# Reordering the loads at the end of two mixture-of-experts stages

## The reference

```
h  = modulate(rms_norm(x, norm_mix), sh1, sc1);  u = split_cols(h @ w_in)      # w_in: 1024 x 2400
x  = x + g1 * (concat(gqa, neighbourhood, differential, latent attention)(u) @ w_out)
h2 = modulate(rms_norm(x, norm_ffn), sh2, sc2)
x  = x + g2 * moe_ffn(h2)
moe_ffn(h) = swiglu(h; shared expert) + sum over 16 experts e: gates[:, e] * swiglu(h; expert e)   # top 2 of 16
swiglu(x, wg, wu, wd) = (silu(x @ wg) * (x @ wu)) @ wd                           # 1024 x 256, 1024 x 256, 256 x 1024
```

## Time and profile before

| | |
|---|---|
| runs | 1728.34, 1732.85, 1733.67 us |
| profiled execution | 1731.82 us, its span 1730.0 us |
| busy shares | TensorE 90%, VectorE 48%, ScalarE 26%, POOL 11% |
| mean granted TensorE clock | 0.966 |
| blocks of layer 0, of layer 1 (us from the start) | about 722 to 964, 1505 to 1696 |

### The profile page before, as it was taken

One profiled execution on the slowest core, in us unless ns is written; L12 is line 12 of the kernel. 1 busy time (PEld: TensorE's weight loads), 2 busy tenths in 40 slices (PEclk: granted clock), 3 DMA queues, 4 the chain that ended last, 5 costly groups with the idle time before them and its releaser, 6 DMA issues.

```text
span 1730.0 us, 24248 instructions
## 1 busy us (share of the span) xinstructions
PE 1561.9 (90%) x8946; PEld 1020.6 (59%) x8946; DVE 827.1 (48%) x1749; ACT 444.1 (26%) x970; POOL 192.8 (11%) x350
## 2 busy tenths in 40 slices
PE   3999999899999999799999489999899999799991
PEld 3655446665665487577677255555565657477771
DVE  1122524567666475255555422434667655444444
ACT  1412113454544210000000142113545531000001
POOL 0110102000000000012211111202000000112112
PEclk7999999999999999899999699999999999899996
DMA  9574230501001589778888820232301123678884
GB/s 336 186 262 146 99 49 1 183 1 38 15 33 40 196 325 390 274 298 316 326 306 314 322 104 4 87 55 63 122 1 37 38 94 128 238 280 305 331 320 165
DMA packets 110485, 295.25 MB, mean 171 GB/s; under 512 B 32568, under 2 KB 42230, under 8 KB 95990
## 3 DMA queue, kind: packets, MB, share of 16 engines
q1 hardware_dynamic: 100022, 272.96, 44.5%
q0 software_dynamic: 10368, 20.99, 3.3%
HBM read 270.72 MB, written 44.04 MB: 182 GB/s over the span
## 4 chain that ended last, share of the span: by engine, by line
PE 82%; DMA 7%; DVE 3%; issue 3%; ACT 3%; SPq 2%; POOL 0%; POOLq 0%; DVEq 0%; ACTq 0%
PE S L1186 16%; PE S L1505 13%; PE B L1319 9%; PE S L1254 9%; PE S L1515 6%; PE PT L1271 5%; PE B L1302 5%; DMA arena<-in_moe_w_up 3%; PE B L1205 3%; PE B L1101 2%; ACT arena L859 2%; PE PT L1499 2%; PE S L1205 2%; PE S L1384 1%; PE PT L1408 1%
## 5 line engine op out<-in xcount | busy, mean ns | idle before, releaser
L1186 PE MATMUL S<-arena 128*128 128x512 f32 (+3 forms) x768 | 301.9, 542 | 13.0 <-ACT arena L859 13.0
L1505 PE MATMUL S<-arena 128*128 128x256 f32 x1152 | 261.3, 384 | 7.2 <-DMA arena<-in_moe_w_up 4.9
L1505 PEld LDWEIGHTS S<-arena 128*128 128x128 f32 x1152 | 220.1, 192 | 55.8 <-issue 27.1
L1186 PEld LDWEIGHTS S<-arena 128*128 128x128 f32 x768 | 141.2, 193 | 137.6 <-issue 105.5
L971 ACT ACTIVATE arena<-S,nmax 128x768 f32<-128x768 f32 (+1 forms) x200 | 161.8, 812 | 159.9 <-DVE nmax L1929 119.7
L1929 DVE TENSOR_REDUCE nmax<-S 128x1 f32<-128x768 f32 (+1 forms) x168 | 133.1, 825 | 84.7 <-PE S L1254 84.5
L1254 PE MATMUL S<-arena 64*128 64x256 f32 (+5 forms) x720 | 161.7, 499 | 9.7 <-ACT arena L971 7.9
L1319 PE MATMUL B<-arena 128*128 128x512 f32 x320 | 156.0, 617 | 2.9 <-DVE arena L1983 2.1
L1271 PEld LDWEIGHTS PT<-cst,arena 128*128 128x128 f32 x832 | 94.0, 141 | 84.2 <-issue 65.4
L1271 PE MATMUL PT<-cst,arena 128*128 128x128 f32 x832 | 121.0, 277 | 24.4 <-ACT arena L971 11.7
L1515 PE MATMUL S<-arena 128*128 128x512 f32 x288 | 129.9, 594 | 2.4 <-DVE arena L2067 2.4
(11 more groups left out here) (282 smaller groups left out, 1703.0 us busy)
## 6 DMA issues: line engine op xcount, KB each, us to landing
arena<-in_w_mod SPq DMA_DIRECT2D x24, 2048.0 KB, 13.3
arena<-in_moe_w_gate SPq DMA_DIRECT2D x36, 1024.0 KB, 5.9
arena<-in_moe_w_up SPq DMA_DIRECT2D x36, 1024.0 KB, 8.9
arena<-in_moe_w_down SPq DMA_DIRECT2D x36, 1024.0 KB
arena<-in_w_in SPq DMA_DIRECT2D x6, 2048.0 KB, 8.4
arena<-y SPq DMA_DIRECT2D x20, 512.0 KB, 7.9
arena<-mod SPq DMA_DIRECT2D x16, 512.0 KB, 16.0
arena<-in_tokens SPq DMA_DIRECT2D x12, 512.0 KB, 9.4
```

Source lines behind the costliest of these rows:

```text
L1186: mm = pe.matmul(ubank[u % 4][:, c0:PANEL_W[p]], hT[:, k, t * P:(t + 1) * P], panel[p][:, k, c0:], start=k == 0, stop=k == KT - 1)
L1505: mm = pe.matmul((S0, S1)[b][:, 512 * w:512 * w + DE], XT[b][:, k, :], wgu[b][:, w, k * DE:(k + 1) * DE], start=k == 0, stop=k == KT - 1)
```

## The change

On SP, in both layers: the loop over `w_load` is split. Blocks 2 and 3 are asked for first, then the residual rows (3 MiB in six loads in layer 0; 2 MiB in four and the gain of 0.5 MiB in layer 1), then in layer 0 panel 0, a wait for `e_y` at 1 (the first block's result scaled), and panel 1, and only then the loop over the weights of blocks 4 and on. `spare_pairs` moves from ahead of the loads of `y` to behind them. In layer 0 the stores to `x_in` wait until all six tiles are summed.

```diff
@@ -794,14 +794,8 @@
                 if l == 0:
                     gain_load(1)
                     mod_store(1)
-                with sp.Fori(0, pairs_1) as i:
-                    for b in range(2):
-
-                        w_load(2 * i + 2 + b, b)
-                if l == 0:
-
-                    win_load(1, 0)
-
+                for b in range(2):
+                    w_load(2 + b, b)
                 for b in range(2):
                     sp.wait_ge(s[f"s_stored{b}"], 8 * gend if l == 0 else 16 * (T // 2 + TL // 2))
                 sp.wait_ge(s["s_d"], gend)
@@ -810,13 +804,18 @@
                 if l == DEPTH - 1:
                     sp.dma_start(fgain, A["final_norm"].partition_broadcast(P)).then_inc(s["c_x_in"], 16)
                 else:
+
+                    win_load(1, 0)
+                    sp.wait_ge(s["e_y"], 1)
                     win_load(1, 1)
+                with sp.Fori(1, pairs_1) as i:
+                    for b in range(2):
+
+                        w_load(2 * i + 2 + b, b)
                 for b in range(2):
 
                     sp.wait_ge(e_stored[l][b], 16 * (pairs_1 + 1))
                     sp.sem_inc(s["spare_seen"], 1)
-                spare_pairs(sp, l, pairs, [("e_gu_in0", 32), ("e_gu_in1", 32), ("e_dn_in0", 16), ("e_dn_in1", 16)])
-
 
                 gc = lambda t: t + T * l
                 dst = (lambda rows: x_in[l + 1][rows, :]) if l < DEPTH - 1 else (lambda rows: out[0, rows, :])
@@ -826,6 +825,10 @@
                         sp.dma_start(y12[t][:, j, :], y_d[l][j * P * nt + t * P:j * P * nt + (t + 1) * P, :]).then_inc(s[f"c_y_in{t}"], 16)
                 if l == 0:
                     small_load(1)
+                spare_pairs(sp, l, pairs, [("e_gu_in0", 32), ("e_gu_in1", 32), ("e_dn_in0", 16), ("e_dn_in1", 16)])
+                if l == 0:
+
+                    sp.wait_ge(s["c_x3"], T)
                 for t in range(nt):
                     sp.wait_ge(s["c_x3"], gc(t) + 1)
                     sp.dma_start(dst(span(t * P, P)), x3[t]).then_inc(s[f"c_stored{t % 2}"], 16)
```

## The result

The changed kernel takes 1752.68 us (median of 4 runs, 1749.63 to 1757.60), the kernel before 1730.59 in the same comparison. The ratio is 1.0128, with a 95% interval of 1.0096 to 1.0159: slower by 17 to 28 us. The forecast was slower, at 1749 in a range of 1739 to 1757, so the sign is right and the median lies in the range; forecast were + 17 us (a sum of + 18, rounded), measured + 22. The profiled execution took 1752.59 us with a span of 1750.7, 20.7 more than before.

What follows compares the result with a forecast made beforehand. TensorE was taken as the bound, DMA (86% busy) a close second. Layer 0's + 13.5 and layer 1's + 4.6 us, together + 18 on 1731.8, gave 1749.9, rounded to 1749 us; range 1739 to 1757.

Steps and rivals of the forecast that it cites:

- Rival (a): Both layers' expert blocks: idle DMA time, 14%, takes the moved loads, no product waits, 1724 us, faster; chance 6%.
- Rival (d): Whole kernel: gains and losses cancel, which needs a layer-0 stall under 6 us; chance 3%.
- Term 1: Layer 0, loads ahead of block 4's weights: 6.69 MB cost 18 us, so block 4's gate product starts 17 us late.
- Term 2: Layer 0, gate product behind the 17 us stall: runs at the lower granted clock, 2.2 us added.
- Term 3: End of layer 0: last scatter without the moved loads, - 2.7 us; `spare_pairs` off the path, - 2.0 us.
- Term 4: Layer 0's stores held until six sums are done: cost 0, covered by VectorE's 21 us idle; gain at most 1.
- Term 5: Layer 1, five loads (2.62 MB) ahead of block 4: stall 4.9 us, clock + 1.7, `spare_pairs` - 2.0.
- Rival (b): Only layer 0 pays: layer 1's stall is 1 to 2 us without clock loss, 1744 or 1741 us; chance 27%.
- Rival (c): Backlog lasts: delayed gathers make blocks 5 and 6 wait too, the layer-0 load cost at its upper end, 1756 us; chance 12%.

## Why the prediction was right

*Mechanism.* The step that decided it, no slack at block 4's weights in layer 0 and one queue, held: the stall is where it was forecast, and it grows with the bytes. Rival (a), that the 14% of idle DMA time takes the loads, is wrong for this order; the spread loads show that the idle time takes most of the rows when they come one per block. Rival (d), gains and losses cancel, is out as well; for a difference under 5 us its condition should have been a stall under 4 us and not under 6, by the forecast's own terms.

*Term 1* was mis-sized: a stall of 17 us, measured 20.34. The highest cost in the text, 20.4 us for the loads, would give a stall of 19.4, less than was measured. The excess goes with the panels. At the forecast's 366 GB/s and 1 us of idle time filled, the rows alone make 7.6 us (measured 7.39), the panels alone 8.7 (11.62), both 17.3 (20.34). Two readings in the forecast can hide it. The 18 us came from a queue observed to its end, whose last 5 us, at a share of 0.27, were counted as 1.35 us of full work; but a product waits for the last byte, and in the changed kernel block 4's weights are such a tail. And SP was to reach block 4's weights at about 765, with the delay inside a full queue. It reached them at 773.63 and the up weights at 779.39, and around that request the queue was not full:

```profile
778.00:780.00 2.00, 0.00 (x0) 0.00 (x0) 0.00 (x0) 0.00 (x0) 0.00 (x0) 0.50 0.69 243
```

How the 3 us divide between the two is open. Not tested was the same load from the queue of another engine, which would keep SP free.

*Term 2*, clock, was 2.2 and 1.7 us, measured 2.6 and 2.9 us.

*Term 3* gave -2.7 and -2.0 in layer 0; measured - 3.4 (5.47 to 2.06) and - 2.1. I took layer 1's 2.81 us as the scatter without a queue; layer 0's is shorter, 2.06 to 2.10 in all ten profiles with rows or panels moved there. With the order of before it took 5.47, 4.67, 5.02 and 4.75 us in four profiles, so the gain is 2.6 to 3.4. Moving either the rows or the panels alone was enough for it.

*Term 4* was 0. VectorE's pause ahead of the units of layer 1 is 21.45 us in both profiles, and the timings show no cost within some 3 us.

*Term 5* was a stall of 4.9 us in layer 1, measured 6.54, 5.79 and 6.01 in three kernels, and 2.9 us of clock where 1.7 were forecast; with both layer 1 cost 7.3 and not 4.6 us. Why this stall is longer is not shown. Rival (b), a stall of 1 to 2 us, is out. Rival (c), more waits behind block 4, did not come as such: behind block 5 of layer 0 the changed kernel has only two waits, 0.98 and 0.67 us, where before there were three and one gate product at the lower clock (5.2 us in all). That is 3.5 us of layer 0's account which the prediction left to its rounding.

Layer 0 in sum: 20.34 - 0.37 (the little wait of before) + 2.6 - 1.0 - 3.5 - 3.4 - 2.1 = 12.6, against a forecast of 13.5. The larger stall and the waits that vanished nearly cancel, so part of the closeness in layer 0 is luck. Over both layers the terms came 2 us short of the profile's 12.6 + 7.3 = 19.9, and rounding down made it 3.

Left open: which of the vanished later waits are due to the change. The kernel before, profiled again with one edit that does not touch the block stage (spare increments, store wait), shows 2.8 us of waits in layer 0 both times, with no gate product behind block 0 at the lower clock, where the first profile has 4.5 and 1.7 more of clock. Against these two the waits that vanished are worth about 1 us and not 4.5, layer 0 would have cost some 3 us more, and most of what brought it to the forecast was the chance of one profile.

## What to carry over

A mean DMA share of 86% says nothing of a lump: before moving loads ahead of weights, read the landing of the very load that will stand behind them and when it is wanted, and look for a stretch where the engines are really idle. Bytes fit where they are small against one block's idle DMA time, or where the queue is empty. Here the rows alone cost 9 us behind block 3's weights, and 31 us earlier nothing that shows: that kernel is 4 to 9 us faster than the one before, spare increments included. A busy queue at the end of a stage costs only what is on the path there (up to 3.4 us here), so the price of clearing it must be smaller.

## What was not expected of the hardware

- A queue of two 1 MiB weight loads behind panels of 1.0 to 1.4 KB pieces ended with the 16 engines 69% busy at 253 GB/s for 10.8 us, where the mean ahead of it was 367.
- SP needed 13.07 us to issue three panel loads while the engines were fully busy, and 5.66 us for the 1 MiB load behind them; the like took 0.34 us in the kernel before.
- Row loads of 4 KB pieces cost 2.3 us of stall per MB, panels 3.3.
- Block 0's gate product of layer 0 took 3.69 us in four profiles and 5.75 to 6.46 in ten. Ahead of it TensorE waits 8 to 11 us for the last `w_mod` load and the granted clock is 0.5; in one profile of the kernel with rows ahead of block 2 the clock was back at 1.00 by 722 us, in the other not until about 726. That is 2.2 us of difference between two executions of one kernel, which no edit made. Times of that kernel spread over 15 us (1719.2 to 1734.2 in 12 runs), so an edit worth 4 us could not be told from none in 12 runs.
